# Depthwise convolution of a streaming encoder on one Trainium2 core: two of 31 taps to GpSimd, five to VectorE, 24 left to TensorE, tap blocks written by GpSimd

## The chip, the cores and the metric

The kernel runs on one core of a Trainium2 chip. The metric is the device time of one execution in microseconds. The core's engines run programs of their own and meet at semaphores: TensorE (matmuls), VectorE, ScalarE, GpSimd, and SyncE, which only issues transfers here. All of them are in order: an instruction that waits holds everything queued behind it on its engine.

## The reference

One step of a two-layer encoder over 256 new frames of one stream and 16 frames of each of 8 running streams, 384 tokens of 1024 channels. The first layer mixes tokens with a causal depthwise convolution of 31 taps (`CONV_K`), between two SwiGLU blocks. The part that matters:

```python
def _conv_module(h, prev, pw1_w, pw1_b, dw_w, dw_b, cln_g, cln_b, pw2_w, pw2_b):
    u = h @ pw1_w + pw1_b
    u = u[..., :D_MODEL] * jax.nn.sigmoid(u[..., D_MODEL:])
    u_full = jnp.concatenate([prev.astype(u.dtype), u], axis=1)
    z = lax.conv_general_dilated(
        u_full, dw_w.astype(u.dtype)[:, None, :], window_strides=(1,), padding='VALID',
        dimension_numbers=('NWC', 'WIO', 'NWC'), feature_group_count=D_MODEL) + dw_b
    z = jax.nn.silu(_layer_norm(z, cln_g, cln_b))
    return z @ pw2_w + pw2_b, u_full[:, -(CONV_K - 1):]
```

The second layer is attention with forget gates over a cache; it and the other blocks are the same in both kernels.

## The kernel before, in words

Channels lie on partitions: the 1024 channels are KT = 8 tiles of 128, each with T = 384 tokens along the free axis (256 of the prompt, 8 x 16 of the streams). All weights come through a ring of four units (`raw`, 512 KB each, issued by SyncE). ScalarE rounds each unit to `wH`, VectorE writes the rest to `wL` (line 1068, `refill`), and TensorE multiplies three times per 128x128 block (`unit`, line 1518; `lead`, line 1526).

The stage of the change runs from about 342 to 442 us. For each tile d of 0 to 7:
- TensorE runs two units of pw1 (a value and a gate half). For d > 2 it then runs `taps(d - 3)`, and after the loop `taps(5)`, `taps(6)`, `taps(7)` (line 1700). Behind d = 4 and d = 6 it multiplies an adaLN block (line 1555), and between the two units of d = 4 stands `shift(1)` (line 1601), the mean of output tile 0.
- ScalarE rounds a unit (line 801), takes the sigmoid of the gate half (line 914), rounds another unit, issues eight of sixteen transfers that copy the tile of u to partitions shifted by 0 to 3 tokens (`shifted_rows`, line 411), and for d > 3 squares output tile d - 4 (line 825).
- VectorE multiplies u = (value + bias) x sigmoid (lines 1361 and 1362), subtracts the rests of two units (line 1068), and evicts an output tile (`conv_out_tile`, line 1351).
- SyncE issues the other eight transfers, the units of the ring and, in `load_taps`, the tap blocks: `taps4` or `tapsT`, 448 KB for each tile, from `cw_d`.

31 taps are seven groups of four (`QUADS`) and three more (`REST`). TensorE does a group of four with one matmul for each 32 channels: the shifted copies of u make a contraction over 4 taps x 32 channels, with a 128x32 block of weights that is diagonal in each quarter. Four such matmuls run beside each other in column groups. `taps(d)` is 7 groups x 2 parts (prompt, streams) x 4 column groups, in float32, so 112 records in the profile. The other three taps are six SCALAR_TENSOR_TENSOR of VectorE (`rest_taps`, lines 1338 to 1343), which build up in `rstd` or `mS`. From tile 1 on they start from minus the shift `cS`, so that the output is already centred; tile 0 is centred by GpSimd (`center`, line 642). `rest_taps(d - 3)` runs ahead of the u of tile d, which leaves tiles 5, 6 and 7 for behind the loop.

GpSimd does `residual(1)` (lines 707 and 709), then sums tiles and squares of tiles for the norm (`add_tile`, lines 656 and 659; `add_square`, lines 665 and 668), each behind a semaphore, and in between copies the last 30 rows of each stream of u for the output (lines 736 and 737). TensorE's `stats(1, ...)` then takes the means (lines 1605 to 1616) and multiplies three adaLN blocks in the gap of the norm, and VectorE normalises.

`taps(d)` waits for its tap blocks, for the shifted copies (`u4_in`), and for output tile d - 2 (its bank is reused). ScalarE's `square(n, k)` writes one of two buffers, and waits for the sum of the square before last.

Of the kernel before, what the change touches and what calls it, by code (L numbers as in the profile page):

```python
# [17 lines left out]
ALU = mybir.AluOpType  # L18
# [17 lines left out]
QUADS = CK // 4  # L36
REST = CK - 4 * QUADS
# [59 lines left out]
_par("dw_rest", REST * KT)  # L97
# [48 lines left out]
def build_program(nc, W, ADA0, ADA, par_d, con_d, x_d, c_d, conv_d, cw_d, kt_d, v_d, lf_d, wf_d,  # L146
                  y_o, kT_o, v_o, lf_o, conv_o, nc_d):
    with ExitStack() as ctx:
# [31 lines left out]
        taps4 = at("taps4", [P, 2, QUADS + 1, P], hid + 4 * KT * UW)  # L180
        o4 = hid + 4 * KT * UW + 8 * (QUADS + 1) * P
# [5 lines left out]
        assert o4 + 56 * UW <= hid + 2 * FT * T * 4  # L187
# [72 lines left out]
        tapsT = at("tapsT", [P, QUADS, P], tmp.manual_sbuf_range[0])  # L260
# [51 lines left out]
        taps_in = [sem(f"taps_in{i}") for i in range(3)]  # L312
        u4_in = [sem(f"u4_in{i}") for i in range(4)]
        silu_done, rest_done = sem("silu_done"), sem("rest_done")
# [16 lines left out]
        TAP_PLACE = ((0, 0), (1, 0), (0, 1), (1, 1), (0, 2), (2, 0), (0, 3), (1, 2))  # L331
# [96 lines left out]
        def _(sp):  # L428
# [99 lines left out]
            load_taps(sp, 1)  # L528
            load_taps(sp, KT - 3)
# [104 lines left out]
        def _(pool):  # L634
# [91 lines left out]
            residual(1)  # L726
            center(1, 0)
            for k in range(1, KT - 1):
                add_tile(1, k)
                add_square(1, k)  # L730
                if k == 4:
                    pool.wait_ge(u_done, 2 + KT)
                    pool.wait_ge(cv_mm, k + 1)
                    for d in range(KT):
                        to = conv_st[:, d] if d < KT - 1 else conv_end[:]
                        g.tensor_copy(to[:, 0:HIST], uF[:, d, SEQ:SEQ + HIST])
                        op = g.tensor_copy(
                            to[:, HIST:].rearrange("p (b t) -> p b t", b=DB),
                            uF[:, d, HIST + SEQ:UROW].rearrange("p (b t) -> p b t", b=DB)[:, :, DS:DS + HIST])
                    op.then_inc(convst_ok, 1)  # L740
# [52 lines left out]
        def _(act):  # L793
# [113 lines left out]
            for d in range(KT):  # L907
# [147 lines left out]
        def _(dve):  # L1055
# [983 lines left out]
```

## Time and profile before

| | us |
|---|---|
| median of 3 runs | 1593.61 |
| lowest and highest | 1590.2 and 1596.02 |
| the profiled execution, its own time | 1590.63 |
| its span, first to last instruction | 1588.8 |
| TensorE busy | 1554.9 (98%) |
| VectorE busy | 796.4 (50%) |
| ScalarE busy | 597.2 (38%) |
| GpSimd busy | 270.1 (17%) |

Times of the trace are microseconds from the span's start. A row in order of time gives the start, the length, the engine, the line of the code, the operation, output and inputs, the number of instructions merged, and in brackets the idle time of the engine before it with what ended it. PE is TensorE, PEld its weight loads, DVE is VectorE, ACT is ScalarE, POOL is GpSimd, SP is SyncE; a q behind the name is the engine's issuing of transfers. Instructions of one engine overlap a little, so a duration is somewhat longer than the step from one start to the next.

### The profile page before, as it was taken

The page shows a single profiled execution, that of the slowest core. Times are in us where ns is not written, and L with a number is a line of the kernel's source. Part 1 is how long each engine was busy: PE and PEld are TensorE (multiplying, and loading weights), DVE is VectorE, ACT ScalarE, POOL GpSimd, SP SyncE. Part 2 cuts the span into 40 slices and gives each one's busy share as a digit, 9 for nine tenths or more (in the row PEclk, how much of TensorE's full clock was granted, in tenths as well). Part 3 has the DMA queues.
Part 4 walks back from the last instruction along what each step waited for, and adds up shares of the span by engine and source line. Part 5 has one row for each costly group of instructions (what it writes and reads, how often), then busy time and mean ns, then how long its engine had stood idle before and what let it go on. Part 6 is the DMA issues. An engine that isn't in the chain of part 4 may idle for free.

```text
span 1588.8 us, 31106 instructions
## 1 busy us (share of the span) xinstructions
PE 1554.9 (98%) x12546; PEld 1493.7 (94%) x12546; DVE 796.4 (50%) x1247; ACT 597.2 (38%) x904; POOL 270.1 (17%) x311
## 2 busy tenths in 40 slices
PE   6999999999999999999999999999998999999998
PEld 5999999998889999999998999999997799999997
DVE  3433345475588434344663534344567684444444
ACT  2432333342255333333353433332346554333332
POOL 1100003260335000012240000003152052000121
PEclk9999999999999999999999999999999999999999
DMA  9555466569883455556417554566556724433441
GB/s 372 179 168 179 165 206 231 181 242 285 259 342 101 167 193 180 196 198 236 163 57 251 197 175 158 189 222 239 194 211 250 284 93 132 132 121 118 145 142 44
DMA packets 86748, 301.66 MB, mean 190 GB/s; under 512 B 10784, under 2 KB 14160, under 8 KB 85328
## 3 DMA queue, kind: packets, MB, share of 16 engines
q1 hardware_dynamic: 83440, 294.55, 54.1%
q10 hardware_dynamic: 3216, 5.80, 1.3%
q8 instruction: 68, 1.11, 0.3%
q14 instruction: 24, 0.20, 0.0%
HBM read 283.31 MB, written 6.32 MB: 182 GB/s over the span
## 4 chain that ended last, share of the span: by engine, by line
PE 88%; DVE 4%; issue 3%; ACT 2%; DMA 1%; POOL 1%; SPq 1%; ACTq 0%; DVEq 0%; POOLq 0%
PE bank L1518 71%; PE bank L1526 8%; PE bank L1555 4%; PE bank L1762 2%; DVE wL L1068 1%; DMA land<-ADA 1%; ACT wH L801 1%; PE bank L1700 1%; PE bank L1855 1%; PE bank L1826 1%; DVE z L1103 0%; PE bank L1797 0%; DVE z L1110 0%; SPq L504 0%; DVE xa L1096 0%
## 5 line engine op out<-in xcount | busy, mean ns | idle before, releaser
L801 ACT ACTIVATE wH<-raw 128x1024 fp32r<-128x1024 f32 x328 | 345.5, 1058 | 507.2 <-PE bank L1518 470.0
L1518 PE MATMUL bank<-hH,wH 128*128 128x384 f32 x1496 | 502.8, 336 | 0.8 <-DVE wL L1068 0.8
L1068 DVE TENSOR_TENSOR wL<-raw,wH 128x1024 fp32r<-128x1024 f32 x328 | 416.6, 1296 | 170.9 <-ACT wH L801 168.0
L1518 PE MATMUL bank<-hH,wL 128*128 128x384 f32 x1496 | 500.0, 334 | 0.0
L1518 PE MATMUL bank<-hL,wH 128*128 128x384 f32 x1496 | 499.7, 334 | 0.0
L1518 PEld LDWEIGHTS bank<-hH,wH 128*128 128x128 f32 x1496 | 280.8, 188 | 5.0 <-DVE wL L1068 2.4
L1518 PEld LDWEIGHTS bank<-hL,wH 128*128 128x128 f32 x1496 | 280.8, 188 | 0.4
L1518 PEld LDWEIGHTS bank<-hH,wL 128*128 128x128 f32 x1496 | 280.8, 188 | 0.0
L1251 DVE TENSOR_TENSOR tmp<-sg,bank 128x384 f32<-128x384 f32 x88 | 48.7, 553 | 432.0 <-PE bank L1518 414.3
L1518 PE MATMUL bank<-hidH,wH 128*128 128x384 f32 x704 | 235.9, 335 | 0.0
L1518 PE MATMUL bank<-hidH,wL 128*128 128x384 f32 x704 | 235.3, 334 | 0.0
L1518 PE MATMUL bank<-hidL,wH 128*128 128x384 f32 x704 | 235.2, 334 | 0.0
L642 POOL TENSOR_TENSOR z<-z,cS 128x384 f32<-128x384 f32 x7 | 8.1, 1155 | 884.8 <-ACT cS L813 884.8
L870 ACT ACTIVATE sg<-bank 128x384 f32<-128x384 f32 x88 | 43.3, 492 | 254.5 <-PE bank L1518 235.5
L1518 PEld LDWEIGHTS bank<-hidH,wH 128*128 128x128 f32 x704 | 132.1, 188 | 1.2 <-issue 0.6
L1518 PEld LDWEIGHTS bank<-hidL,wH 128*128 128x128 f32 x704 | 132.1, 188 | 0.0
L1518 PEld LDWEIGHTS bank<-hidH,wL 128*128 128x128 f32 x704 | 132.1, 188 | 0.0
L1526 PE MATMUL bank<-hH,wH 128*128 128x384 f32 x232 | 80.2, 346 | 5.5 <-DVE wL L1068 2.7
L1526 PE MATMUL bank<-hH,wL 128*128 128x384 f32 x232 | 78.3, 337 | 0.0
L1526 PE MATMUL bank<-hL,wH 128*128 128x384 f32 x232 | 78.2, 337 | 0.0
L668 POOL TENSOR_TENSOR sqs<-sqs,sqb 128x384 f32<-128x384 f32 x34 | 50.1, 1475 | 150.3 <-ACT sqb L825 150.3
L1526 PEld LDWEIGHTS bank<-hH,wH 128*128 128x128 f32 x232 | 44.1, 190 | 9.6 <-DVE hL L1206 5.2
(234 smaller groups left out, 1569.1 us busy)
## 6 DMA issues: line engine op xcount, KB each, us to landing
raw<-W SPq DMA_DIRECT2D x328, 512.0 KB, 3.9
araw<-ADA SPq DMA_DIRECT2D x52, 512.0 KB, 5.4
gapZ<-ADA SPq DMA_DIRECT2D x36, 512.0 KB, 5.5
land<-ADA SPq DMA_DIRECT2D x16, 512.0 KB, 15.2
gapE<-ADA SPq DMA_DIRECT2D x16, 512.0 KB, 4.2
KTb<-kt_d SPq DMA_DIRECT2D x8, 1024.0 KB, 7.2
Vb<-v_d SPq DMA_DIRECT2D x8, 1024.0 KB, 5.2
gapH<-ADA SPq DMA_DIRECT2D x12, 512.0 KB, 4.6
```

The source lines that it names most:

```text
L668: g.tensor_tensor(sqs[:], sqs[:], sqb[:, k % 2], ALU.add).then_inc(sqs_done, 1)
L801: a.activation(wH[:, slot, :], raw[:, slot, :], ACT.Copy).then_inc(w_hi, 1)
L870: a.activation(sg[:, j, :], bank[2 * j][:, 0:T], ACT.Silu).then_inc(sg_done, 1)
L1068: v.tensor_tensor(wL[:, slot, :], raw[:, slot, :], wH[:, slot, :].bitcast(F32), ALU.subtract)\
L1251: v.tensor_tensor(tmp[:, j, :], sg[:, j, :], bank[2 * j + 1][:, 0:T], ALU.mult)\
L1518: op = mm(out, tile_w(w, slot, k), m[:, k0 + k, :], start=start and k == 0 and q == 0, stop=stop and k == nk - 1 and q == 2)
L1526: op = mm(bank[j][:, 0:T], tile_w(w, j, k), m[:, k, :], start=k == 0 and q == 0, stop=k == KT - 1 and q == 2)
L1555: op = mm(out[32 * j:32 * j + 32, 0:cols], cact[:, k, :], tile[:, cols * j:cols * j + cols], start=start, stop=stop)
L1700: op = mm(acc, weights[:, q, rows], src, start=q == 0, stop=q == QUADS - 1)
L1762: op = mm(bank[4 * half + t][:, :], h[:, k, tok], w[:, j, 512 * kk:512 * kk + 512], start=k == 0 and q == 0, stop=k == KT - 1 and q == 2)
L1826: op = nc.tensor.transpose(bank[4 + half][:, c * P:c * P + P], prS[buffer(n, half)][:, c0:c0 + P], ident)
L1855: op = mm(bank[6][32 * kk:32 * kk + 32, cols], turned_p[:, half, c0:c0 + 32], V, start=t == 0, stop=t == 2)
```

## The change

VectorE takes five taps of each tile and GpSimd two; TensorE keeps six groups of four.
- The tap blocks are no longer loaded. One transfer brings the taps of all tiles (192 columns) and a 32x32 identity per quarter (`tapw`). `make_taps(d)` multiplies both with repetition, one TENSOR_TENSOR of 128x768 on GpSimd, into one of three places.
- `inner_taps(d)` on GpSimd multiplies u by tap 24 into `z[:, d]` and by tap 25 into `rstd`, in two parts each, and adds them. `rest_taps(d)` of VectorE waits for that and adds taps 26 to 30 in `z[:, d]`.
- `shift_taps(d)` on GpSimd subtracts the shift `cS` from `z[:, d]` for d from 1. `conv_out_tile(d)` waits for it.
- VectorE runs `rest_taps(0)`, `(1)` and `(2)` in the iterations 1 to 3 and `rest_taps(d)` in iteration d from 3, behind the evicted tile; none is left behind the loop.
- GpSimd's queue gets a new order, written out. The copies for the output come behind `shift_taps(7)`.

The diff, with declarations and the packing of the inputs left out:

```diff
-QUADS = CK // 4
-REST = CK - 4 * QUADS
+QUADS = 6
+INNER = 2
+REST = CK - 4 * QUADS - INNER
...
-            s = TAP_PLACE[d][0]
-            return tapsT[:] if s == 2 else taps4[:, s, 0:QUADS]
-        def load_taps(queue, d):
-            queue.dma_start(tap_tile(d), cw_d[d].rearrange("p (q c) -> p q c", q=QUADS))\
-                .then_inc(taps_in[TAP_PLACE[d][0]], 16)
+            return tapsT[:] if d % 3 == 2 else taps4[:, d % 3, 0:QUADS * P]
+        def two_parts(ap):
+            return ap[:, 0:SEQ], ap[:, SEQ:T].rearrange("p (b t) -> p b t", b=DB)
...
-                if 2 < d < KT - 1:
-                    sp.wait_ge(cv_mm, d - 2)
-                    load_taps(sp, d - 1 if d < KT - 2 else KT - 1)
-            load_taps(sp, 0)
-            load_taps(sp, 1)
-            load_taps(sp, KT - 3)
+            sp.dma_start(tapw[:], cw_d).then_inc(taps_in, 16)
...
+            def make_taps(d):
+                if d == 0:
+                    pool.wait_ge(taps_in, 16)
+                elif d > 2:
+                    pool.wait_ge(cv_mm, d - 2)
+                n = 4 * QUADS
+                g.tensor_tensor(tap_tile(d).rearrange("p (n c) -> p n c", n=n),
+                                tapw[:, n * d:n * d + n].unsqueeze(2).to_broadcast([P, n, 32]),
+                                tapw[:, n * KT:n * KT + 32].unsqueeze(1).to_broadcast([P, n, 32]), ALU.mult)\
+                    .then_inc(taps_made, 1)
+            def inner_taps(d):
+                pool.wait_ge(xa_done, KT + d + 1)
+                pool.wait_ge(u_done, 2 + d + 1)
+                for q, to in enumerate((z[:, d], rstd)):
+                    if q == 1 and d > 0:
+                        pool.wait_ge(pool_taps, 3 * d)
+                    for part in range(2):
+                        op = g.tensor_scalar(two_parts(to)[part], window(uF[:, d], 4 * QUADS + q)[part],
+                                             pcol("dw_rest", KT * q + d), None, ALU.mult)
+                    op.then_inc(pool_taps, 1)
+                pool.wait_ge(pool_taps, 3 * d + 2)
+                g.tensor_tensor(z[:, d, :], z[:, d, :], rstd[:], ALU.add).then_inc(pool_taps, 1)
+            def shift_taps(d):
+                pool.wait_ge(cs_done, 2)
+                pool.wait_ge(rest_done, 2 * REST * (d + 1))
+                g.tensor_tensor(z[:, d, :], z[:, d, :], cS[:], ALU.subtract).then_inc(taps_moved, 1)
+            make_taps(0)
+            inner_taps(0)
+            inner_taps(1)
+            make_taps(1)
+            inner_taps(2)
+            make_taps(2)
+            inner_taps(3)
+            make_taps(3)
+            shift_taps(1)
             center(1, 0)
-            for k in range(1, KT - 1):
+            shift_taps(2)
+            for d in range(4, KT):
+                inner_taps(d)
+                make_taps(d)
+                add_tile(1, d - 3)
+                add_square(1, d - 3)
+                shift_taps(d - 1)
+            shift_taps(KT - 1)
+            for t in range(KT):
+                to = conv_st[:, t] if t < KT - 1 else conv_end[:]
+                g.tensor_copy(to[:, 0:HIST], uF[:, t, SEQ:SEQ + HIST])
+                op = g.tensor_copy(
+                    to[:, HIST:].rearrange("p (b t) -> p b t", b=DB),
+                    uF[:, t, HIST + SEQ:UROW].rearrange("p (b t) -> p b t", b=DB)[:, :, DS:DS + HIST])
+            op.then_inc(convst_ok, 1)
+            for k in range(5, KT - 1):
                 add_tile(1, k)
                 add_square(1, k)
-                if k == 4:
-                    pool.wait_ge(u_done, 2 + KT)
-                    pool.wait_ge(cv_mm, k + 1)
-                    for d in range(KT):
-                        to = conv_st[:, d] if d < KT - 1 else conv_end[:]
-                        g.tensor_copy(to[:, 0:HIST], uF[:, d, SEQ:SEQ + HIST])
-                        op = g.tensor_copy(
-                            to[:, HIST:].rearrange("p (b t) -> p b t", b=DB),
-                            uF[:, d, HIST + SEQ:UROW].rearrange("p (b t) -> p b t", b=DB)[:, :, DS:DS + HIST])
-                    op.then_inc(convst_ok, 1)
...
-                if d == KT - 1:
-                    act.wait_ge(cv_mm, KT - 3)
-                    load_taps(act, KT - 2)
...
-                total = (rstd, mS)[d % 2]
-                acc = (total[:, 0:SEQ], total[:, SEQ:T].rearrange("p (b t) -> p b t", b=DB))
-                shift = (cS[:, 0:SEQ], cS[:, SEQ:T].rearrange("p (b t) -> p b t", b=DB))
+                acc = two_parts(z[:, d])
+                dve.wait_ge(pool_taps, 3 * d + 3)
+                for q in range(REST):
+                    w = pcol("dw_rest", KT * (INNER + q) + d)
+                    for part in range(2):
+                        src = window(uF[:, d], 4 * QUADS + INNER + q)[part]
+                        if q > 0:
+                            dve.wait_ge(rest_done, 2 * REST * d + 2 * q + part - 1)
+                        v.scalar_tensor_tensor(acc[part], src, w, acc[part], ALU.mult, ALU.add).then_inc(rest_done, 1)
+            def conv_out_tile(d):
+                dve.wait_ge(cv_mm, d + 1)
                 if d > 0:
-                    dve.wait_ge(cs_done, 2)
-                if d > 1:
-                    dve.wait_ge(z_ready, 2 + KT + d - 1)
-                for q in range(REST):
-                    w = pcol("dw_rest", KT * q + d)
-                    for part in range(2):
-                        src = window(uF[:, d], 4 * QUADS + q)[part]
-                        if q == 0 and d == 0:
-                            op = v.tensor_scalar(acc[part], src, w, None, ALU.mult)
-                        elif q == 0:
-                            op = v.scalar_tensor_tensor(acc[part], src, w, shift[part], ALU.mult, ALU.subtract)
-                        else:
-                            dve.wait_ge(rest_done, 2 * REST * d + 2 * q + part - 1)
-                            op = v.scalar_tensor_tensor(acc[part], src, w, acc[part], ALU.mult, ALU.add)
-                        op.then_inc(rest_done, 1)
-            def conv_out_tile(d):
-                dve.wait_ge(cv_mm, d + 1)
-                dve.wait_ge(xa_done, KT + d + 1)
-                dve.wait_ge(rest_done, 2 * REST * (d + 1))
-                v.scalar_tensor_tensor(z[:, d, :], bank[4 + d % 2][:, 0:T], pcol("dw_b", d), (rstd, mS)[d % 2][:],
+                    dve.wait_ge(taps_moved, d)
+                else:
+                    dve.wait_ge(rest_done, 2 * REST)
+                v.scalar_tensor_tensor(z[:, d, :], bank[4 + d % 2][:, 0:T], pcol("dw_b", d), z[:, d, :],
                                        ALU.add, ALU.add).then_inc(z_ready, 1)
             for d in range(KT):
                 j, n = d % 2, U_PW1 + 2 * d
-                if d > 2:
-                    rest_taps(d - 3)
                 dve.wait_ge(sig_done, d + 1)
                 A = bank[2 * j]
                 uP, uS = window(uF[:, d], HIST)
@@ -1366,12 +1396,13 @@
                 refill(n + RING + 1, 2 * j + 1)
                 if d > 2:
                     conv_out_tile(d - 3)
-            rest_taps(KT - 3)
+                if 0 < d < 4:
+                    rest_taps(d - 1)
+                if d > 2:
+                    rest_taps(d)
             conv_out_tile(KT - 3)
-            rest_taps(KT - 2)
+            modulation(B_CONV)
             conv_out_tile(KT - 2)
-            modulation(B_CONV)
-            rest_taps(KT - 1)
             conv_out_tile(KT - 1)
             normalise(1, (M_PW2, h32, hH, hL), B_CONV_GAP, bank[3])
...
-                place, use = TAP_PLACE[d]
-                weights = tap_tile(d)
-                pe.wait_ge(taps_in[place], 16 * use + 16)
+                weights = tap_tile(d).rearrange("p (q c) -> p q c", q=QUADS)
+                pe.wait_ge(taps_made, d + 1)
                 pe.wait_ge(u4_in[d % 4], 256 * (d // 4) + 256)
                 pe.wait_ge(z_ready, 2 + KT + d - 1)
...
```

## Rows read from the trace of the kernel before

**Rows 1.** The page's first part: busy time, share of the span, instructions

```profile
PE 1554.9 (98%) x12546; PEld 1493.7 (94%) x12546; DVE 796.4 (50%) x1247; ACT 597.2 (38%) x904; POOL 270.1 (17%) x311
```

**Rows 2.** TensorE's waits, 342 to 443 us: waiting and releaser, us, times, longest

```profile
PE bank L1605 <- POOL zs L659: 1.3, 1, 1.3
...
PE bank L1700 <- DMA taps<-cw_d: 0.5, 1, 0.5
```

**Rows 3.** The chain that ended last: start, us, what (the stage's first pieces)

```profile
345.85 16.89 PE bank L1518 x96
362.73 4.69 PE bank L1700 x112
```

**Rows 4.** TensorE in order of time: the shift, the last taps, the norm's gap

```profile
371.62 0.81 PE L1601 MATMUL bank<-z,con 128*128 128x384 f32 x2
...
436.73 0.27 PE L1700 MATMUL bank<-u_low,taps 128*32 128x128 f32 x1
...
445.36 0.97 PE L1555 MATMUL bank<-gapL,cact 128*32 128x128 f32 x28 [1.12 <-issue]
```

**Rows 5.** VectorE in order of time: refills, u tiles and taps

```profile
351.88 2.85 DVE L1068 TENSOR_TENSOR wL<-raw,wH 128x1024 fp32r<-128x1024 f32 x2
...
367.55 0.48 DVE L1361 SCALAR_TENSOR_TENSOR uF<-bank,par,sg 128x256 f32<-128x256 f32 x1 [3.61 <-ACT sg L914]
...
377.25 0.48 DVE L1361 SCALAR_TENSOR_TENSOR uF<-bank,par,sg 128x256 f32<-128x256 f32 x1 [0.41 <-ACT sg L914]
...
391.33 0.48 DVE L1361 SCALAR_TENSOR_TENSOR uF<-bank,par,sg 128x256 f32<-128x256 f32 x1 [6.52 <-ACT sg L914]
...
392.00 2.35 DVE L1068 TENSOR_TENSOR wL<-raw,wH 128x1024 fp32r<-128x1024 f32 x2
...
395.97 0.74 DVE L1340 SCALAR_TENSOR_TENSOR mS<-uF,par,cS 128x256 f32<-128x256 f32 x2
396.63 1.40 DVE L1343 SCALAR_TENSOR_TENSOR mS<-uF,par,mS 128x256 f32<-128x256 f32 x4
...
418.63 0.48 DVE L1361 SCALAR_TENSOR_TENSOR uF<-bank,par,sg 128x256 f32<-128x256 f32 x1 [6.52 <-ACT sg L914]
```

**Rows 6.** GpSimd in order of time: residual, sum of squares, copies, last sum

```profile
351.89 0.55 POOL L707 TENSOR_SCALAR xa<-z,gA,bP 128x256 f32<-128x256 f32 x1
352.43 2.47 POOL L709 TENSOR_SCALAR xa<-z,gA,bA 128x128 f32<-128x128 f32 x1
...
398.40 1.01 POOL L665 TENSOR_TENSOR sqs<-sqb 128x384 f32<-128x384 f32 x1 [23.03 <-ACT sqb L825]
...
432.03 0.20 POOL L736 COPY conv_st<-uF 128x30 f32<-128x30 f32 x1
...
432.50 0.20 POOL L736 COPY conv_st<-uF 128x30 f32<-128x30 f32 x1
...
438.15 0.99 POOL L668 TENSOR_TENSOR sqs<-sqs,sqb 128x384 f32<-128x384 f32 x1
```

**Rows 7.** Line 645 of GpSimd: its instructions, ns least, median, most

```profile
L645 POOL TENSOR_TENSOR xa<-xa,cS x8: 1834/2343/2852, 242.7 to 1502.8; 128x768 f32<-128x768 f32 x8
```

**Rows 8.** ScalarE in order of time: eight transfers issued, a square

```profile
359.93 5.96 ACTq L411 DMA_DIRECT2D u<-uF  x8
...
397.73 0.53 ACT L825 ACTIVATE sqb<-z 128x384 f32<-128x384 f32 x1 [5.48 <-issue]
```

**Rows 9.** All engines in order of time at 428 us: VectorE beside GpSimd

```profile
427.80 1.00 POOL L659 TENSOR_TENSOR zs<-zs,z 128x384 f32<-128x384 f32 x1
427.82 2.29 DVE L1340 SCALAR_TENSOR_TENSOR rstd<-uF,par,cS 128x256 f32<-128x256 f32 x2
...
428.76 1.19 POOL L668 TENSOR_TENSOR sqs<-sqs,sqb 128x384 f32<-128x384 f32 x1
```

**Rows 10.** Stretches: PE, PEld, DVE, ACT, POOL busy, granted clock, DMA share, GB/s

```profile
29.00:30.00 1.00, 0.00 (x0) 0.00 (x0) 0.31 (x1) 0.59 (x1) 0.00 (x0) 1.00 1.04 414
33.00:34.00 1.00, 1.00 (x5) 1.00 (x4) 0.00 (x0) 0.92 (x2) 0.74 (x2) 0.50 1.06 404
```

More of the change, by code:

```diff
@@ L96 @@
 _par("dw_b", KT)
-_par("dw_rest", REST * KT)
+_par("dw_rest", (INNER + REST) * KT)
 _par("b_f", 1)
@@ L179, in build_program @@
         uF = at("uF", [P, KT, UW], hid)
-        taps4 = at("taps4", [P, 2, QUADS + 1, P], hid + 4 * KT * UW)
-        o4 = hid + 4 * KT * UW + 8 * (QUADS + 1) * P
+        taps4 = at("taps4", [P, 2, UNIT], hid + 4 * KT * UW)
+        o4 = hid + 4 * KT * UW + 8 * UNIT
         conv_in = at("conv_in", [P, KT, DB, HIST], o4)
@@ L186, in build_program @@
         assert o4 + 4 * KT * DB * HIST <= hid + 3 * BLK and o4 + 4 * (KT - 1) * HIST * NG <= hid + 3 * BLK
-        assert o4 + 56 * UW <= hid + 2 * FT * T * 4
+        tapw = at("tapw", [P, KT * 4 * QUADS + 32], o4 + 56 * UW)
+        assert o4 + 56 * UW + 4 * (KT * 4 * QUADS + 32) <= hid + 2 * FT * T * 4
         kvH = at("kvH", [P, KT, T], hid, F32R)
@@ L259, in build_program @@
         om = at("om", [P, 2, P], epS.manual_sbuf_range[0])
-        tapsT = at("tapsT", [P, QUADS, P], tmp.manual_sbuf_range[0])
+        tapsT = at("tapsT", [P, QUADS * P], tmp.manual_sbuf_range[0])
+        assert tmp.manual_sbuf_range[0] + 4 * QUADS * P <= zs.manual_sbuf_range[0]
         sg_off = sg.manual_sbuf_range[0]
@@ L311, in build_program @@
             "hist_ok", "sig_done", "u_done", "cv_mm", "convst_ok"))
-        taps_in = [sem(f"taps_in{i}") for i in range(3)]
+        taps_in, taps_made = sem("taps_in"), sem("taps_made")
         u4_in = [sem(f"u4_in{i}") for i in range(4)]
-        silu_done, rest_done = sem("silu_done"), sem("rest_done")
+        silu_done, rest_done, pool_taps, taps_moved = (sem(n) for n in (
+            "silu_done", "rest_done", "pool_taps", "taps_moved"))
         kf_done, vs_done, f_mm, lf_chain, ncum_done, lfo_done = (sem(n) for n in (
@@ L1324, in rest_taps @@
             def rest_taps(d):
-                total = (rstd, mS)[d % 2]
-                acc = (total[:, 0:SEQ], total[:, SEQ:T].rearrange("p (b t) -> p b t", b=DB))
-                shift = (cS[:, 0:SEQ], cS[:, SEQ:T].rearrange("p (b t) -> p b t", b=DB))
-                if d > 0:
-                    dve.wait_ge(cs_done, 2)
-                if d > 1:
-                    dve.wait_ge(z_ready, 2 + KT + d - 1)
+                acc = two_parts(z[:, d])
+                dve.wait_ge(pool_taps, 3 * d + 3)
                 for q in range(REST):
-                    w = pcol("dw_rest", KT * q + d)
+                    w = pcol("dw_rest", KT * (INNER + q) + d)
                     for part in range(2):
-                        src = window(uF[:, d], 4 * QUADS + q)[part]
-                        if q == 0 and d == 0:
-                            op = v.tensor_scalar(acc[part], src, w, None, ALU.mult)
-                        elif q == 0:
-                            op = v.scalar_tensor_tensor(acc[part], src, w, shift[part], ALU.mult, ALU.subtract)
-                        else:
+                        src = window(uF[:, d], 4 * QUADS + INNER + q)[part]
+                        if q > 0:
                             dve.wait_ge(rest_done, 2 * REST * d + 2 * q + part - 1)
-                            op = v.scalar_tensor_tensor(acc[part], src, w, acc[part], ALU.mult, ALU.add)
-                        op.then_inc(rest_done, 1)
+                        v.scalar_tensor_tensor(acc[part], src, w, acc[part], ALU.mult, ALU.add).then_inc(rest_done, 1)
             def conv_out_tile(d):
                 dve.wait_ge(cv_mm, d + 1)
-                dve.wait_ge(xa_done, KT + d + 1)
-                dve.wait_ge(rest_done, 2 * REST * (d + 1))
-                v.scalar_tensor_tensor(z[:, d, :], bank[4 + d % 2][:, 0:T], pcol("dw_b", d), (rstd, mS)[d % 2][:],
+                if d > 0:
+                    dve.wait_ge(taps_moved, d)
+                else:
+                    dve.wait_ge(rest_done, 2 * REST)
+                v.scalar_tensor_tensor(z[:, d, :], bank[4 + d % 2][:, 0:T], pcol("dw_b", d), z[:, d, :],
                                        ALU.add, ALU.add).then_inc(z_ready, 1)
@@ L1953, in _tap_blocks @@
     taps[:] = w[:4 * QUADS]
-    cw = np.zeros((KT, 4, 32, QUADS, 4, 32), np.float32)
-    c = np.arange(32)
-    cw[:, :, c, :, :, c] = taps.reshape(QUADS, 4, KT, 4, 32).transpose(4, 2, 1, 0, 3)
-    return cw.reshape(KT, P, QUADS * P)
+    of = taps.reshape(QUADS, 4, KT, 4, 32).transpose(1, 4, 2, 0, 3).reshape(P, KT * 4 * QUADS)
+    return np.concatenate([of, np.tile(np.eye(32, dtype=np.float32), (4, 1))], 1)
 def _constants():
@@ L1993 @@
     put("dw_b", _cols(i["dw_b"]))
-    put("dw_rest", np.concatenate([_cols(i["dw_w"][0][4 * QUADS + q]) for q in range(REST)], 1))
+    put("dw_rest", np.concatenate([_cols(i["dw_w"][0][4 * QUADS + q]) for q in range(INNER + REST)], 1))
     par[0:H, PAR["b_f"][0]] = i["b_f"]
```

1 line of the change is left out of this document (removed).

## The prediction

> **What bounds the kernel now.** I read the page first: TensorE is busy 98% of the span [rows 1], so elsewhere only its own work or its gaps count. The change touches one stage, the convolution between 342 and 442 us. There I read the waits of TensorE [rows 2]: 0.5 us for a transfer of tap blocks and 1.3 us for GpSimd's sum at the end are the largest that belong to the taps. The stage is now TensorE's, with thin edges. Then I read each engine's order of time around one tile, since the change puts two engines into one chain of waits, and last the place where VectorE and GpSimd run together.
>
> A unit of weights takes TensorE 4.2 us (four in 16.89), tap blocks of one tile 4.7 us [rows 3]. So a tile costs 8.4 + 4.7 = 13.1 us, some 14 with an adaLN block, and the u tiles of VectorE come at that pace (391.33 after 377.25, VectorE idle for 6.5 us before it) [rows 5].
>
> **TensorE.** Six groups of seven remain: 4.7/7 = 0.67 us less for each of 8 tiles, 5.3 us. The 0.5 us wait for a tap block [rows 2] goes with the eight 448 KB loads. So at most 5.8 us can be won, if nothing else becomes late.
>
> **VectorE.** A tap costs two instructions, 0.66 us together (four in 1.40, two in 0.74, each with some 0.07 of overlap [rows 5]). Five taps are 3.3 us for each tile, where three were 2.0. Against 13 us for a tile that alone is hidden.
>
> **GpSimd.** Per tile: the tap blocks are one instruction of 128x768 elements with two repeated operands. The trace has none; the nearest is L645, 128x768 with one repeated operand, 1.83 us at the least [rows 7]. Bounds: 1.0 us (what 128x384 takes) and 2.8 us (L645's longest [rows 7]); I take 1.83. The two inner taps are four TENSOR_SCALAR like L707 and L709 (0.54 us from the one at 351.89 to the next, some 0.43 for the shorter one), 1.94 us, and a sum of 1.0 us as at 438.15 [rows 6], so 3.0 us. shift_taps is another 1.0 us, the sums of tiles and squares 1.0 each as before. In all 7.9 us for a tile of 12.4: by busy time it fits. Two things in the trace say that it doesn't.
>
> **One: the order of GpSimd's queue.** For d from 4, GpSimd makes inner_taps(d), make_taps(d), add_tile(d-3), add_square(d-3), shift_taps(d-1). ScalarE makes square d-3 one tile later, behind its transfers of tile d+1: 397.73 stands behind 5.5 us of issuing [rows 8], and GpSimd sat idle 23 us until it [rows 6]. Today nobody waits for that. After the change inner_taps(d+1) is queued behind it, VectorE's rest_taps(d+1) waits for inner_taps, and the u of tile d+2 is queued behind rest_taps on VectorE. That closes a loop from u(d+1) to u(d+2): eight transfers issued 5.3, square 0.45, add_square 1.0, shift_taps 1.0, inner_taps 3.0, five taps 3.3, u 0.7, handovers 0.3: 15.0 us, where TensorE now needs 12.4 or 13.4. It is run from u(5) to u(7) and once more to the end.
>
> **Two: VectorE and GpSimd shut each other out.** At 427.8 both start at once: the two L1340 take 2.29 us where they take 0.74 at 395.97, and L668 beside them takes 1.19 instead of 0.99 [rows 5, 6, 9]. In the same way L709 at 352.43 takes 2.47 us, across the two VectorE refills from 351.88 [rows 5, 6]. So an instruction of VectorE with two operands in SBUF and one of GpSimd alternate, and their times add. The taps and refills are such instructions, and so is all of GpSimd's new work.
>
> The Trainium skill says the same in "SBUF — State Buffer", section "Who interferes with whom": a VectorE instruction with two SBUF inputs and a GpSimd instruction that reads SBUF block each other for their whole length. [...] By that rule the result is the likeliest case below, without it the first rival; the row of 2.29 us agrees with the rule.
>
> **The walk.** I took each engine's queue in order with the durations above, times on the scale of before. GpSimd is free at 354.9 [rows 6]. make 1.8 and inner(0) 3.0: 359.7. VectorE, done with its refills at 354.7 [rows 5], stands waiting in rest_taps(0) and then alternates with inner(1) and make(1): 3.3 + about 4 us, so u(2) is written at 368, where today its transfers start at 359.9. ScalarE cannot start on tile 3 before it has issued those (5.96 us [rows 8]), and VectorE has refills 2.35, taps 3.3 and GpSimd's inner(2) and make(2) in between: u(3) at 378 instead of 368. Behind it two refills and the first output tile, 381. For that tile TensorE waits in shift(1), which it passed at 371.6 [rows 4]: it is held up 7.6 us there and 2.6 us before it for a refill. rest_taps(2) and (3), 6.6 us, alternate with 6 us of GpSimd: u(4) at 394 (378 before). inner(4) and make(4): u(5) at 405 (392) [rows 5].
>
> Now the loop. With make_taps taking the port before the first tap (1.8 us) and some alternation it is 17.3 us instead of 15.0: u(6) at 422.4, u(7) at 439.7 (419.3 before [rows 5]). The end: square 445.5, add_square and shift 447.5, inner(7) 450.5, make(7) 452.3, taps of VectorE among three GpSimd sums 458, output tile 5 at 458.5. TensorE's taps(7) waits for that and ends at 462.6 (437.0 before [rows 4]). GpSimd meanwhile copies the state, 0.47 us for each tile, 3.8 in all [rows 6], and then still owes four sums of 1.0: 466.6, against 439.1 now (438.15 and 0.99 [rows 6]). The statistics follow at once, as now. That is +27.5 us.
>
> Two corrections. After the stage TensorE sits idle 1.1 us for a transfer of an adaLN piece (445.36 [rows 4]); those land long before: -1.1. And TensorE will stand still for about 10 us before taps(7). The trace shows what follows an idle stretch: around 29 us TensorE stood idle, and at 33 the granted clock was 0.50, the lower level of 1.2 GHz, from 31.8 to 35.2 in all [rows 10]. At half pace 3.4 us do the work of 1.7: +1.7 in taps(7). What the earlier stalls cost so is hidden, since TensorE isn't late there.
>
> Sum: 1590.6 (the profiled execution; its span is 1588.8) + 27.5 - 1.1 + 1.7 = 1618.7, say 1619 us. The median of the runs shown, 1593.6, is 3.0 above the profiled one; the range carries that.
>
> **Nothing hides this.** The stages behind are TensorE's at 98%, and all of them wait for the norm of this stage.
>
> **Bounds.** Tap blocks at 1.0 us instead of 1.83 give -6.4 us in the walk, at 2.8 us +8. The second clock drop, at the statistics, would be +1.7. If the inner taps took GpSimd a fifth less, -3. So the likeliest case has 1608 to 1632.
>
> **Rivals.**
> First, the loop without the exclusion (or with little of it): 15.0 us per tile, and the early delays nearly vanish, since VectorE and GpSimd overlap. u(5) at about 390, u(6) 405, u(7) 420, inner(7) 430.5, taps(7) from 434.4 to 438.4, GpSimd's last sum at 444: +5, and up to +14 where half the exclusion counts: 1596 to 1605. Against it speak [rows 9]; for it, that only two places of the trace show the exclusion at full length.
> Second, the other side: TensorE stays the bound and the change gives its full 5.8 us, 1585. It needs every u at most 12.4 us behind the one before, and GpSimd's last sum no later than 434. It decides at the square: if ScalarE had each square out before GpSimd reaches the sum of it, the loop would fall to some 8 us. [rows 6] speak against it: GpSimd had waited 23 us there.
> Third, losses and gains cancel (within 0.3%): about 1593. For that the loop would have to run at 13 us.
> Fourth, worse than the walk: tap blocks with two repeated operands at twice L645, 3.7 us, give +15 on top, 1634.
>
> **Chances.** The walk 0.63, the first rival 0.17, the second 0.09, the third 0.05, the fourth 0.06. What a measurement can tell from no change is about 0.3%, 4.8 us. Faster 0.09; same 0.05 and a sliver of the first rival, 0.07; slower 0.84. The range takes in the walk with its bounds and most of the first rival: 1599 to 1633.
>
> **What would show it.** Right: TensorE idle before the mean matmul of shift(1) (L1601 now) and before taps(7), VectorE's first tap of a tile waiting for GpSimd, u tiles 17 us apart from 5 to 7, GpSimd's sums of squares waiting for ScalarE at d = 4 to 7, single VectorE taps of about 1 us and more, granted clock below 1 in the stage. Wrong: u tiles 12.4 us apart (then the second rival), or 15 us apart with taps of 0.4 us (the first). The length of the tap-block instruction on GpSimd is the number that I know least; each 0.1 us of it is worth 0.8 us.

## The result and the profile after

The changed kernel takes 1617.1 us, median of 4 runs (1616.6 to 1621.9), against 1592.9 for the kernel before; the ratio is 1.0166, with a 95% interval of 1.0154 to 1.0177. It is 24 us slower by the medians and 26 us by the ratio. The profiled execution took 1616.8 us with a span of 1614.8 us, 26.0 us more than the span of before.

From the page of the changed kernel, TensorE's busy time, as in [rows 1]:

```profile
PE 1556.1 (96%) x12418; PEld 1492.8 (92%) x12418; DVE 817.1 (51%) x1279; ACT 597.7 (37%) x904; POOL 330.1 (20%) x366
```

Its waits between 340 and 480 us answer to [rows 2]. The columns are the waiting line, its releaser, us in total, times, the longest:

```profile
PE bank L1730 <- DVE z L1383: 20.1, 2, 10.4
PE bank L1632 <- DVE z L1383: 6.5, 1, 6.5
PE bank L1636 <- POOL zs L655: 0.9, 1, 0.9
...
```

L1730 is the tap matmuls, L1632 the mean matmul of shift(1), L1636 the statistics, and L1383 is VectorE's output of a tile. Before, the largest wait of this kind was 1.3 us. Now TensorE stands still for 6.5 us in shift(1), 9.7 before taps(6) and 10.4 before taps(7). In order of time, TensorE (start, us, operation, count, idle time ahead with its releaser):

```profile
377.22 1.65 PE L1632 MATMUL bank<-z,con 128*128 128x384 f32 x2 [6.45 <-DVE z L1383]
...
440.86 6.15 PE L1730 MATMUL bank<-u,taps 128*32 128x256 f32 x96 [9.70 <-DVE z L1383]
...
457.44 0.61 PE L1730 MATMUL bank<-u_own,taps 128*32 128x256 f32 x1 [10.44 <-DVE z L1383]
...
464.77 0.88 PE L1636 MATMUL bank<-zs,con 128*128 128x384 f32 x2 [0.94 <-POOL zs L655]
```

VectorE (L1374 is the five taps, two instructions each; the first of each u tile is L1391; L1383 the output of a tile), to be read beside [rows 5]:

```profile
360.06 3.89 DVE L1374 SCALAR_TENSOR_TENSOR z<-uF,par,z 128x256 f32<-128x256 f32 x10 [5.89 <-POOL z L748]
363.87 0.47 DVE L1391 SCALAR_TENSOR_TENSOR uF<-bank,par,sg 128x256 f32<-128x256 f32 x1
...
388.14 0.47 DVE L1391 SCALAR_TENSOR_TENSOR uF<-bank,par,sg 128x256 f32<-128x256 f32 x1
...
399.66 0.47 DVE L1391 SCALAR_TENSOR_TENSOR uF<-bank,par,sg 128x256 f32<-128x256 f32 x1
...
413.59 5.35 DVE L1374 SCALAR_TENSOR_TENSOR z<-uF,par,z 128x256 f32<-128x256 f32 x10 [10.41 <-POOL z L748]
418.86 0.47 DVE L1391 SCALAR_TENSOR_TENSOR uF<-bank,par,sg 128x256 f32<-128x256 f32 x1
...
437.19 0.47 DVE L1391 SCALAR_TENSOR_TENSOR uF<-bank,par,sg 128x256 f32<-128x256 f32 x1
...
449.98 6.79 DVE L1374 SCALAR_TENSOR_TENSOR z<-uF,par,z 128x256 f32<-128x256 f32 x10 [9.27 <-POOL z L748]
456.69 0.60 DVE L1383 SCALAR_TENSOR_TENSOR z<-bank,par,z 128x384 f32<-128x384 f32 x1
```

Tiles 5, 6 and 7 of u are 19.2 and 18.3 us apart (399.66, 418.86, 437.19). VectorE sits idle for 10.4 us of such a turn, until GpSimd's inner taps are there. What GpSimd does in that turn (L661 sum of squares, L754 shift_taps, L744 inner taps, L748 their sum, L731 the tap blocks), and ScalarE before it (L414 the eight transfers, L868 the square), are the rows to read beside [rows 6] and [rows 8]:

```profile
400.42 6.36 ACTq L414 DMA_DIRECT2D u<-uF  x8
406.83 0.52 ACT L868 ACTIVATE sqb<-z 128x384 f32<-128x384 f32 x1 [8.09 <-issue]
```

```profile
407.50 1.02 POOL L661 TENSOR_TENSOR sqs<-sqb 128x384 f32<-128x384 f32 x1 [10.94 <-ACT sqb L868]
408.46 1.02 POOL L754 TENSOR_TENSOR z<-z,cS 128x384 f32<-128x384 f32 x1
409.46 1.51 POOL L744 TENSOR_SCALAR z<-uF,par 128x256 f32<-128x256 f32 x2
410.94 1.52 POOL L744 TENSOR_SCALAR rstd<-uF,par 128x256 f32<-128x256 f32 x2
412.54 1.02 POOL L748 TENSOR_TENSOR z<-z,rstd 128x384 f32<-128x384 f32 x1
413.51 1.49 POOL L731 TENSOR_TENSOR tapsT<-tapw 128x768 f32<-128x768 f32 x1
...
464.58 0.99 POOL L664 TENSOR_TENSOR sqs<-sqs,sqb 128x384 f32<-128x384 f32 x1
```

The turn can be read off these rows: u(5) at 399.66, transfers issued 400.42 to 406.8, square, sum of squares at 407.50, shift, inner taps 409.46 to 413.5, VectorE's taps 413.59 to 418.9, u(6) at 418.86. GpSimd was idle for 10.9 us and VectorE for 10.4 us of it: neither is short of time, each waits for the other and both for ScalarE.

### The profile page after: what moved, and what is told of

Its sections match the earlier page's. It is cut to its first block, busy times and chain, and to the rows that moved or that the text cites. A ratio compares the mean times of both kernels' runs of the same rounds, so it can differ in the third digit from the quotient of the medians.

```text
span 1614.8 us, 30938 instructions
## 1 busy us (share of the span) xinstructions
PE 1556.1 (96%) x12418; PEld 1492.8 (92%) x12418; DVE 817.1 (51%) x1279; ACT 597.7 (37%) x904; POOL 330.1 (20%) x366
## 3 DMA queue, kind: packets, MB, share of 16 engines
q10 hardware_dynamic: 3072, 5.35, 1.3%
## 4 chain that ended last, share of the span: by engine, by line
PE 85%; DVE 6%; issue 3%; POOL 2%; ACT 2%; DMA 1%; SPq 1%; ACTq 0%; DVEq 0%; POOLq 0%
PE bank L1549 69%; PE bank L1557 8%; PE bank L1586 3%; DVE z L1374 1%; DVE wL L1108 1%; PE bank L1792 1%; DMA land<-ADA 1%; ACT wH L844 1%; PE bank L1885 1%; PE bank L1856 1%; DVE hL L1246 0%; POOL z L744 0%; DVE z L1143 0%; PE bank L1827 0%; ACTq L414 0%
## 5 line engine op out<-in xcount | busy, mean ns | idle before, releaser
L1549 PEld LDWEIGHTS bank<-hH,wH 128*128 128x128 f32 x1496 | 281.1, 188 | 5.5 <-issue 2.5
L868 ACT ACTIVATE sqb<-z 128x384 f32<-128x384 f32 x56 | 28.5, 515 | 94.7 <-issue 46.2
```

Of the source, the lines that this page charges most:

```text
L868: a.activation(sqb[:, k % 2], z[:, k, :], ACT.Square).then_inc(sq_done, 1)
L1549: op = mm(out, tile_w(w, slot, k), m[:, k0 + k, :], start=start and k == 0 and q == 0, stop=stop and k == nk - 1 and q == 2)
```

## Experiments

The four kernels e1, e2, e3 and e5 were measured beside one set of runs of the kernel before (1591.1 us), e4, e6 and e7 beside another (1592.6 us), e8 beside a third (1592.2 us). The times move by 1 or 2 us between sets, so small differences are taken from the ratios; 0.001 of the ratio is 1.6 us.

### The sums come two tiles later (e1_lag)

Theory: the loop over ScalarE's square sets the pace. Rival: VectorE and GpSimd are slow by the work that they do.

```diff
             for d in range(4, KT):
+                if d > 5:
+                    add_tile(1, d - 5)
+                    add_square(1, d - 5)
                 inner_taps(d)
                 make_taps(d)
-                add_tile(1, d - 3)
-                add_square(1, d - 3)
                 shift_taps(d - 1)
             shift_taps(KT - 1)
+            for k in (3, 4):
+                add_tile(1, k)
+                add_square(1, k)
```

> The changed kernel with one edit in GpSimd's queue: the sums of tile and square d-5 ahead of inner_taps(d), instead of those of d-3 behind make_taps(d); 3 and 4 stand behind shift_taps(7). Theory (a loop through GpSimd's wait for ScalarE's square, with exclusion between VectorE and GpSimd): the loop is cut, what is left from one u to the next is inner taps 4.0, refills 2.3 and taps 5.3 in turn, 12.5 us; the early delay stays (u(4) at 389, u(5) at 400), u(7) at about 426 instead of 438, GpSimd's last sum at 451 instead of 466: 1603 us. Rival (only the port time counts, the order doesn't): u tiles stay 18 to 19 us apart, 1617 us, at most 3 less.

1605.4 us (1604.6 to 1606.1), ratio 1.0084 (1.0069 to 1.0099). No operation was removed, and 11.7 us went (13 us by the ratios). VectorE's refills follow each u tile at once and show its pace; behind them stands GpSimd's first inner tap:

```profile
401.50 2.34 DVE L1112 TENSOR_TENSOR wL<-raw,wH 128x1024 fp32r<-128x1024 f32 x2
...
407.85 6.09 DVE L1378 SCALAR_TENSOR_TENSOR z<-uF,par,z 128x256 f32<-128x256 f32 x10 [3.48 <-POOL z L748]
...
414.52 2.34 DVE L1112 TENSOR_TENSOR wL<-raw,wH 128x1024 fp32r<-128x1024 f32 x2
```

```profile
401.75 3.47 POOL L744 TENSOR_SCALAR z<-uF,par 128x256 f32<-128x256 f32 x2 [3.61 <-DVE uF L1396]
```

The turns are 12.3, 13.0 and 13.8 us. The loop is shown. A smaller one is left: u(d), inner taps of d on GpSimd, VectorE's taps of d, u(d+1). In it VectorE waits 3.5 us for GpSimd, and GpSimd's first pair of taps takes 3.47 us instead of 1.51, since it starts beside the refills. TensorE still waits 5.4 us in shift(1), 5.2 us before taps(7) and 4.7 us for GpSimd's last sum.

### Inner taps as multiply and add (e2_two_op)

The inner taps are TENSOR_SCALAR with one operation, and took 1.51 us for a pair where the prediction had 0.97 from rows with two operations [rows 6]. The edit adds an operation that changes nothing. Theory: the form itself is slow. Rival: the taps are slow from their shifted operand or from VectorE beside them.

```diff
-                                             pcol("dw_rest", KT * q + d), None, ALU.mult)
+                                             pcol("dw_rest", KT * q + d), 0.0, ALU.mult, ALU.add)
```

> The changed kernel with one edit: the inner taps multiply and add 0.0 (two operations in one instruction, as residual(1) does) instead of only multiplying. In the profile the one-operation form took 0.90 and 0.60 us from start to start, the two-operation form of residual(1) 0.54 and 0.43. Theory (the form is what costs): inner taps fall from 4.0 to 3.0 us, each turn of the loop and the start lose 1 us: five to six us less, 1611 us. Rival (the form is the same, u as input is what costs): nothing changes, 1617 us.

1611.5 us, ratio 1.0122 (1.0107 to 1.0137), 5.6 us less than the changed kernel (7.0 us by the ratios). The pairs on GpSimd, in order of time:

```profile
408.47 0.83 POOL L744 TENSOR_SCALAR z<-uF,par 128x256 f32<-128x256 f32 x2
409.28 0.83 POOL L744 TENSOR_SCALAR rstd<-uF,par 128x256 f32<-128x256 f32 x2
```

0.83 us instead of 1.51: the form was the cost, and the turns fall to 17.6 and 17.2 us. The gain lies in the turns and behind them. At the start nothing is won: VectorE's first ten taps, 3.89 us in the changed kernel, take 6.13 us here, with GpSimd's sum and tap block now beside them too, and u(2) comes at 364.8 instead of 363.9:

```profile
358.74 6.13 DVE L1374 SCALAR_TENSOR_TENSOR z<-uF,par,z 128x256 f32<-128x256 f32 x10 [4.36 <-POOL z L748]
```

### Tap blocks filled with zeros (e3_fill)

Two fills take the place of the multiplication that reads SBUF; the blocks hold zeros, so TensorE's part of the convolution is left out of the output. GpSimd is busy about as long. Theory: VectorE's taps beside make_taps are slow because GpSimd reads. Rival: GpSimd's time alone matters.

```diff
-                g.tensor_tensor(tap_tile(d).rearrange("p (n c) -> p n c", n=n), ..., ALU.mult)\
-                    .then_inc(taps_made, 1)
+                g.memset(tap_tile(d), 0.0).then_inc(taps_filled, 1)
+                pool.wait_ge(taps_filled, d + 1)
+                g.memset(tap_tile(d), 0.0).then_inc(taps_made, 1)
```

> The changed kernel with GpSimd's product for the tap blocks replaced by two memsets of the same place, one behind the other (estimate from the memset of 128x512 in the trace of before, 0.52: 0.75 us each, 1.5 together, as long as the product). The blocks are zero, so the part of TensorE's taps is left out of the result; its matmuls run as before. GpSimd is as busy but reads no SBUF there. Theory (VectorE's two-operand instructions are shut out by GpSimd instructions that read): the first tap of a tile takes 0.5 us instead of 1.69, each turn loses 1.2 to 1.5 us, in all 5 to 8: 1610 us. Rival (GpSimd's queue time is what counts, or any GpSimd instruction shuts VectorE out): unchanged, 1617 us within 2.

1612.2 us, ratio 1.0124 (1.0108 to 1.014), 4.9 us less (6.7 us by the ratios). The five taps of tile 5, that took 5.35 us at 413.59 above:

```profile
411.87 4.13 DVE L1373 SCALAR_TENSOR_TENSOR z<-uF,par,z 128x256 f32<-128x256 f32 x10 [9.63 <-POOL z L747]
```

What is left above 3.38 (which tile 4 took here) is one sum of GpSimd.

### Tap blocks loaded (e4_loaded)

```diff
+        def load_taps(queue, d):
+            queue.dma_start(tap_tile(d), cw_d[d]).then_inc(taps_in[d % 3], 16)
...
                 inner_taps(d)
-                make_taps(d)
```

> The changed kernel with its six groups, but each tile's block of taps is loaded whole by DMA into one of the three places, as the kernel before loads its block, and GpSimd makes none. Theory (the loop u, square, sums, shift, inner taps, taps is the bound, and make_taps stands in it only through what it holds up: VectorE's taps of the same tile, 4.59 to 5.35 us instead of 3.38): those taps fall to 3.4 to 4.1 us, as where the blocks were filled with zeros (1612.2), and GpSimd is besides free of 1.48 us in each turn, which runs beside VectorE's taps and ends before them. So 1610 to 1613 us, the same as with the fill, if the eight loads of 393 KB land in time. Rival (making the blocks is GpSimd work in series with the loop): 8 x 1.48 us less, 1605 us. Second rival (the loads delay the shifted rows or the weights on SyncE's queue): 1617 us or more, with TensorE's wait at the taps on a DMA.

1610.8 us, ratio 1.0113 (1.0097 to 1.0128), 6.3 us less than the changed kernel (8.4 us by the ratios). The five taps of tile 5 are as with the zeros:

```profile
410.88 4.11 DVE L1365 SCALAR_TENSOR_TENSOR z<-uF,par,z 128x256 f32<-128x256 f32 x10 [9.47 <-POOL z L744]
```

To be rid of all 12 us that GpSimd spends on tap blocks brings only 1.4 us more than to be rid of its reads (1.8 us by the ratios, and the two intervals overlap). The rival had 1605 us, 12 us less in all. So make_taps stood in the path almost only through VectorE's taps, and no load was late: TensorE has no wait for a transfer there.

### Both edits (e7_lag_two_op)

> Both earlier edits together: the sums of GpSimd come two tiles later (1605.4 us alone) and the inner taps are multiply-and-add with 0 (1611.5 us alone, 5.6 us less than the changed kernel). Theory (one loop sets the pace; once the late sums have opened it, the pace of the u tiles is TensorE's, 12.3 to 13.8 us, and GpSimd's inner taps are hidden but for the first tiles and the last): the two do not add up, 1602 to 1605 us. Rival (the inner taps cost their 1 us in every turn whatever the sums do): the gains add, 1599.8 us or less.

1601.7 us (1600.4 to 1604.4), ratio 1.0057 (1.0041 to 1.0073): 4.3 us below e1 by the ratios (0.0027 of 1592), of the 5.6 to 7.0 us that the edit brought alone. It lies between the two expectations, and the rows decide against my theory:

```profile
400.82 2.34 DVE L1112 TENSOR_TENSOR wL<-raw,wH 128x1024 fp32r<-128x1024 f32 x2
...
405.81 6.11 DVE L1378 SCALAR_TENSOR_TENSOR z<-uF,par,z 128x256 f32<-128x256 f32 x10 [2.11 <-POOL z L748]
...
412.49 2.34 DVE L1112 TENSOR_TENSOR wL<-raw,wH 128x1024 fp32r<-128x1024 f32 x2
```

The turn is 11.7 us where e1 had 13.0, and VectorE's wait 2.1 where it was 3.5: 1.3 us less in both. So e1 ran at the pace of the small loop, and not, as I had said, at TensorE's. What is left here stands before and behind the loop: TensorE waits 6.0 us in shift(1) and 7.0 us for GpSimd's last sum.

### All seven taps on VectorE (e5_seven)

The small loop exists because one engine's tap work stands behind another's. Here GpSimd has none, and tiles from 4 on take the shift in VectorE's first tap. Not shown: GpSimd's sums are in a late order like that of e1.

```diff
-INNER = 2
+INNER = 0
...
-                dve.wait_ge(pool_taps, 3 * d + 3)
+                dve.wait_ge(u_done, 2 + d + 1)
...
+                        elif q == 0:
+                            op = v.scalar_tensor_tensor(acc[part], src, w, two_parts(cS)[part], ALU.mult, ALU.subtract)
```

> Seven taps on VectorE, none on GpSimd, TensorE six groups, tap blocks by GpSimd; from tile 4 on the first tap starts from minus the shift, for tiles 1 to 3 GpSimd subtracts it; sums of tiles and squares never ahead of what VectorE waits for. Theory: no chain of VectorE through GpSimd is left, VectorE has 14 taps of 0.33 us, 4.6 us for a tile, so TensorE is the bound: 5.3 us less of matmuls, 0.5 us of waiting for a block and up to 1 us at the end: 1586 to 1588 us where before has 1592.9. Rival (the time of GpSimd's blocks and VectorE's added taps on the shared port is enough to lose the gain): 1592 to 1596 us, TensorE waiting for output tiles.

1594.9 us (1592.4 to 1598.4, 12 runs), ratio 1.0020 (1.0011 to 1.0028). 22 us of the loss are gone. Part of that is the late order of the sums; against e1, which has it too, it is 10 us less. But the gain did not come: the rival was right. TensorE's waits, and two rows of VectorE (L1361, L1365 taps):

```profile
PE bank L1623 <- DVE z L1374: 4.9, 1, 4.9
PE bank L1721 <- DVE z L1374: 3.8, 1, 3.8
```

```profile
354.89 4.91 DVE L1361 TENSOR_SCALAR z<-uF,par 128x256 f32<-128x256 f32 x2
...
430.20 8.15 DVE L1365 SCALAR_TENSOR_TENSOR z<-uF,par,z 128x256 f32<-128x256 f32 x12
```

The first taps of tile 0 are held for 4.9 us by GpSimd's making of blocks, with u(2) behind them; the last taps take 8.15 us instead of 4.03 beside GpSimd's sums, with the output of tile 5 behind them.

### The same, in another order (e6_order)

Against e5. Not shown: GpSimd's sums come one tile earlier, and tile 3 too takes the shift in VectorE's first tap, so that this is not a change of order alone.

```diff
-                if 0 < d < 4:
-                    rest_taps(d - 1)
+                if d == 2:
+                    rest_taps(0)
+                if d == 3:
+                    rest_taps(1)
                 if d > 2:
-                    rest_taps(d)
+                    rest_taps(d - 1)
             conv_out_tile(KT - 3)
+            rest_taps(KT - 1)
```

> The kernel with seven taps on VectorE and none on GpSimd (1594.9 us), with only its order changed: the rest taps of tile d follow u of tile d+1 instead of standing ahead of it (tile 0 after u(2), tiles 1 and 2 after u(3), then tile d-1 after u(d)), the output of tile 5 stands ahead of the taps of tile 7, and GpSimd's sums come one tile earlier, so that fewer lie beside the last taps. Theory (the 4.9 us wait at shift(1) and the 3.8 us wait at taps(7) are all that keeps TensorE's gain of 5 to 6 us from the end): both waits go, and the time is 1586 to 1589 us, below the kernel before (1591.1 to 1592.9). Rival (something else is late next, such as the sums that GpSimd ends after the last output, or VectorE's taps beside them): 1591 to 1595 us, with TensorE's waits at the stats or at taps(7) instead.

1592.2 us (11 runs), ratio 1.0002 (0.9993 to 1.0011): no difference from before, so the rival again. The 4.9 us are gone. What is late next:

```profile
PE bank L1629 <- POOL zs L655: 3.0, 1, 3.0
PE bank L1723 <- DVE z L1373: 2.4, 1, 2.4
```

```profile
422.83 6.67 DVE L1364 SCALAR_TENSOR_TENSOR z<-uF,par,z 128x256 f32<-128x256 f32 x12
429.42 0.60 DVE L1373 SCALAR_TENSOR_TENSOR z<-bank,par,z 128x384 f32<-128x384 f32 x1
430.84 5.91 DVE L1364 SCALAR_TENSOR_TENSOR z<-uF,par,z 128x256 f32<-128x256 f32 x12
```

Twelve instructions that take 4.03 us alone take 6.67 and 5.91 beside GpSimd's sums and copies; the output of tile 5 (429.42) and GpSimd's sum of tile 6 come late by that.

### A version below both kernels (e8_best)

Against e6. Besides what the diff shows, GpSimd's copies of the state come behind its sums, and TensorE takes tile 6 into the norm itself.

```diff
-                if d > 2:
+                if 2 < d < 6:
                     rest_taps(d - 1)
+                if d in (5, 6):
+                    rest_taps(d)
+            rest_taps(KT - 1, 0, 4)
             conv_out_tile(KT - 3)
-            rest_taps(KT - 1)
+            rest_taps(KT - 1, 4)
...
-        SUMMED = [KT - 1 if n == 2 else KT for n in range(7)]
+        SUMMED = [KT - 1 if n in (1, 2) else KT for n in range(7)]
```

> The reordered kernel with seven taps on VectorE (1592.2 us), whose rows show what is late: TensorE waits 2.4 us ahead of taps(7) for the output of tile 5, since VectorE's taps of tile 6 beside three of GpSimd's operations took 6.67 us instead of 4.03, and 3.0 us at the norm for GpSimd's sum of tile 6, since the taps of tile 7 took 5.91 us. Edits: VectorE does the taps of tiles 5 and 6 each one turn earlier, in its idle time behind u(5) and u(6); the taps of tile 7 are cut into four ahead of the output of tile 5 and three behind it; GpSimd sums tiles 1 to 5 only and TensorE takes tile 6 itself with two matmuls (0.44 us each); GpSimd's copies of the state come behind its sums. Theory (those two waits are the rest of the gain): both go, 5.4 us less and 0.9 us more for the matmuls, 1586 to 1589 us, below the kernel before by 3 to 6 us. Rival (the 48 matmuls for the modulation and the weights of the next stage come in at the same time whenever the norm ends, so that an earlier norm only moves the wait behind it): 1590 to 1593 us, with a wait of TensorE for DMA behind the norm.

1585.1 us (1584.7 to 1586.8, 5 runs), ratio 0.9961 (0.9947 to 0.9974): 7.1 us below the kernel before by the medians (6.2 us by the ratio) and 32 us below the changed one. TensorE's waits from 340 to 480 us are these; both large ones are gone, and the wait for a transfer behind the norm, of which the rival spoke, is 0.6 us:

```profile
PE bank L1543 <- DVE wL L1088: 0.8, 1, 0.8
PE bank L1580 <- DMA gapC<-ADA: 0.6, 1, 0.6
PE bank L1626 <- DVE z L1371: 0.2, 1, 0.2
```

The norm's last matmul ends 5.3 us earlier than before (436.1 for 441.4). That equals the gain of the six groups, but other terms cancel in it: the wait of 1.3 us for GpSimd's sum [rows 2] is gone, and the norm has two more matmuls of tile 6, which take 1.3 us. What each of the four edits is worth was not taken apart.

## Why the prediction was right

It gave 1619 us, from 1599 to 1633, and 84% for slower; the measured median is 1617.1 us. Its sum was made against the profiled execution of before and gave 1618.7, where the profiled execution of after took 1616.8. Point by point:

- **TensorE's own gain** (5.8 us at most): right in size. A tile's taps at full clock take 4.08 us (at 384.55) for 4.73 before (at 377.42), 0.65 us less, 5.2 us for eight tiles, and e8 brings about as much to the end of the norm. It could not show in the changed kernel.
- **The loop** (one): right, shown by e1. It was put at 17.3 us with the exclusion and is 19.2 and 18.3 us. The terms: issuing took 6.4 and 5.6 us for 5.3; the inner taps 4.1 us for 3.0; VectorE's taps with make_taps in them 5.3 us for 5.1 (3.3 + 1.8) and the some 0.5 of further alternation in the 17.3. The inner taps are the term that is mis-sized in both turns; issuing adds as much in the first one. I took the rows of L707 and L709 [rows 6], which have the same operands and shape but two operations, and thought one to be no dearer; e2 prices the difference at 5.6 to 7.0 us of the kernel's time.
- **The tap blocks**: 1.48 us for 1.83, inside the bounds of 1.0 and 2.8. The sentence that each 0.1 us is worth 0.8 us was wrong. Without the 1.48 us of each block the kernel is 6.3 to 8.4 us faster (e4), some 0.4 to 0.6 us for each 0.1, and nearly all of it comes where GpSimd reads beside VectorE's taps.
- **The exclusion** (two): right in the loop for the tap blocks, shown by e3 and e4, and too general as a rule, see the next point. The Trainium skill's rule ("SBUF — State Buffer", "Who interferes with whom") is that such a VectorE instruction and a GpSimd instruction that reads SBUF shut each other out, and that one that only writes doesn't; the fill of e3, which writes only, left VectorE's taps 1.2 us shorter (4.13 for 5.35 us). That trace agrees with both halves. The changed kernel's first taps do not agree with the first half, and there the measurement decides: GpSimd's inner taps read SBUF too, and the two ran side by side.
- **The early delays** were put too high. The walk's times are those at which a u tile is written, 0.65 us behind the start of its first row: u(2) at 368, u(3) at 378, u(4) at 394; measured 364.5, 373.0 and 388.8. The step that failed is "3.3 + about 4 us" for VectorE's first taps: the ten, which take 3.38 us alone, took 3.89 us beside GpSimd's inner taps. There the two times did not add up. VectorE lost 0.5 us and GpSimd 0.6 us in its four instructions, the first two of which are this pair of tile 1, which takes 1.51 us alone:

```profile
360.00 1.80 POOL L744 TENSOR_SCALAR z<-uF,par 128x256 f32<-128x256 f32 x2
```

- **These two errors cancelled, by luck.** The 4.7 us less at u(5) (400.3 for 405) stand against 1.8 and 1.0 us more in the two turns and 0.9 us more behind u(7) (27.7 for 26.9). There the inner taps took 1.1 us more than walked and the square came 0.3 us later, but VectorE's last taps took 6.8 us where the walk has 7.5. The last sum of GpSimd ends at 465.6 (464.58 and 0.99), predicted 466.6. The time is nearer than its parts deserved.
- **The wait for an adaLN piece** (-1.1): right, no wait for a transfer is among TensorE's waits above.
- **The clock** (+1.7): the cause was right and the term wrong. Four stretches of the changed kernel (us, PE, PEld, DVE, ACT, POOL busy with counts, granted clock, DMA share, GB/s), to be read beside [rows 10]:

```profile
374.00:379.00 5.00, 1.78 (x4) 1.18 (x5) 5.00 (x9) 0.10 (x1) 5.00 (x4) 0.50 0.90 279
381.00:433.00 52.00, 50.15 (x704) 43.14 (x702) 28.55 (x47) 10.42 (x14) 28.14 (x28) 1.00 0.62 178
436.00:444.00 8.00, 3.15 (x32) 1.76 (x36) 4.71 (x9) 0.67 (x2) 0.06 (x1) 0.50 0.55 150
453.00:460.00 7.00, 2.56 (x25) 1.37 (x29) 5.46 (x12) 1.05 (x2) 4.74 (x13) 0.50 1.02 416
```

  Each of the three long waits of TensorE has its stretch at 0.50, the lower level of 1.2 GHz, and between the first and the second the clock is full. taps(6) took 6.15 us for 4.1 and taps(7) some 6.4 us. But behind taps(7) TensorE still waits 0.94 us for GpSimd's last sum. So the slower clock costs nothing at the end there: the walk already ended with GpSimd, and adding 1.7 us to it counted a time that lies beside it. Without that term the sum is 1617.0, for 1616.8 measured, which is again nearer than its parts.
- **The rivals**: "without the exclusion" was to be 1596 to 1605 us. It was tested only in part: e3 and e4 take away the exclusion by make_taps and no other. What the exclusion by GpSimd's sums and by VectorE's refills is worth in the changed kernel is not shown. The "other side" named 1585 us and the square as the point from which it decides. e1 moved the square out of the way and reached 1605.4, not 1585: the square was the first barrier and not the only one.

## What to carry to other kernels

Work that fits an engine by busy time can still close a loop: follow the queues from one output of a stage to the next one, over every engine, and compare the sum of that path with the bound's time for one tile. A step that two engines share in series puts both their queues, and all that stands in these, into the path; give the step to one engine, and place it behind the instructions that others wait for. Where VectorE and GpSimd read SBUF at once, plan with the sum of their times close to a deadline (it is the safe bound: some pairs here overlapped), and move GpSimd's sums and copies away from it.

## What the hardware showed beyond that

- On GpSimd a TENSOR_SCALAR with one operation is slower than with two. Over the stage (line, operation, count, busy us, mean ns, idle time before), first the changed kernel, then the one with multiply and add:

```profile
L744 POOL TENSOR_SCALAR rstd<-uF,par 128x256 f32<-128x256 f32 x6 | 6.0, 1008 | 0.0
L744 POOL TENSOR_SCALAR rstd<-uF,par 128x128 f32<-128x128 f32 x6 | 4.3, 715 | 0.0
```

```profile
L744 POOL TENSOR_SCALAR rstd<-uF,par 128x256 f32<-128x256 f32 x5 | 2.7, 545 | 0.0
L744 POOL TENSOR_SCALAR rstd<-uF,par 128x128 f32<-128x128 f32 x5 | 1.9, 387 | 0.0
```

  1.01 against 0.55 us, and 0.72 against 0.39.
- VectorE's TENSOR_SCALAR with a single tile as operand is held by GpSimd too: two of them took 4.91 us beside make_taps (e5 at 354.89), and 0.53 us at 366.61 of the same trace.
- Which of the two engines pays depends on the instructions and on how they meet. Ten taps of VectorE took 3.89 us beside one-operation inner taps of GpSimd and 5.35 us beside its tap block and a sum, for 3.38 alone. One pair of inner taps took 3.47 us beside VectorE's two refills. And in e6 GpSimd paid for nearly all: two of its subtractions, 1.0 us each when alone, took 6.90 us, while the twelve taps of VectorE beside them (at 376.98) kept their 4.03 us. What decides it isn't settled by these runs.

```profile
376.94 6.90 POOL L740 TENSOR_TENSOR z<-z,cS 128x384 f32<-128x384 f32 x2
```
